# Weight sums of a coming FFN made in the preceding mixer or PLE gate, second-stage tiles among them

## What is computed

```python
for i in range(DEPTH):                                  # DEPTH = 2
    x = x + 0.5 * swiglu(rmsnorm(x, norm_ffn[i, 0]), w_ffn_gate_up[i, 0], w_ffn_down[i, 0])
    h = rmsnorm(x, norm_mix[i])
    mix = even_mixer(h, ...) if i % 2 == 0 else odd_mixer(h, ...)
    x = x + mix
    x = x + 0.5 * swiglu(rmsnorm(x, norm_ffn[i, 1]), w_ffn_gate_up[i, 1], w_ffn_down[i, 1])
    gate = sigmoid(rmsnorm(x, norm_ple[i]) @ w_ple_gate[i])
    x = x + gate * rmsnorm(p[i] @ w_ple_proj[i], norm_ple_proj[i])
y = rmsnorm(x, norm_final)
```

## Time and profile before

| | us |
|---|---|
| median of three runs | 2645.11 |
| profiled execution | 2654.71 |
| its span, slowest core (2) | 2653.2 |
| spans of the eight cores | 2618.6 to 2653.2 |
| PE busy | 2448.4 (92%) |
| DVE busy | 1805.2 (68%) |
| ACT busy | 1009.9 (38%) |
| POOL busy | 977.4 (37%) |
| mean granted clock of PE, by core | 0.954 to 0.967 |

### The profile page before, as it was taken

The page is one execution under the profiler, slowest core; times in us unless marked ns, Lnnn a source line. Parts: engine busy times, 40 slices in busy tenths (PEclk is TensorE's granted clock), DMA queues, the critical chain, the costliest instruction groups (busy, mean ns, idle before and its releaser), DMA issues.

```text
span 2653.2 us, 36263 instructions; the slowest of 8 cores (2618.6 to 2653.2 us)
## 1 busy us (share of the span) xinstructions
PE 2448.4 (92%) x13362; PEld 1165.4 (44%) x13449; DVE 1805.2 (68%) x2922; ACT 1009.9 (38%) x1767; POOL 977.4 (37%) x1006
## 2 busy tenths in 40 slices
PE   7788879999998999899898998999999999999997
PEld 3233434545443444454443444454444444455443
DVE  6889664765676687377785776476566868666677
ACT  3233321444762334044551433143333513423344
POOL 1476875211225656530034746510003256211100
PEclk9899989999999999999999999999999999999887
DMA  7585688663455879965055779953311566755513
GB/s 144 123 194 125 117 183 200 151 141 79 113 130 114 180 166 205 209 164 109 7 129 135 174 171 207 208 129 65 62 38 21 116 147 155 172 128 128 110 21 131
DMA packets 115570, 351.57 MB, mean 133 GB/s; under 512 B 15936, under 2 KB 31296, under 8 KB 115264
## 3 DMA queue, kind: packets, MB, share of 16 engines
q0 software_dynamic: 47088, 163.21, 36.9%
q1 hardware_dynamic: 67584, 184.92, 21.5%
q10 hardware_dynamic: 720, 1.11, 0.1%
HBM read 426.51 MB, written 75.63 MB: 189 GB/s over the span
## 4 chain that ended last, share of the span: by engine, by line
PE 61%; DMA 13%; DVE 13%; POOL 6%; issue 3%; ACT 3%; SPq 0%; POOLq 0%; DVEq 0%; ACTq 0%
PE ps L614 61%; DMA stg<-wts 8%; POOL ringh L580 3%; DMA ringh<-wts 3%; DVE scr L577 3%; DVE hh L584 2%; DVE hih L577 2%; POOL stg L580 2%; DMA x<-xT 1%; DVE h L584 1%; ACT scr L571 1%; DVE x L584 1%; DMA ringh<-wsum 1%; DVE ht L577 1%; ACT L569 1%
## 5 line engine op out<-in xcount | busy, mean ns | idle before, releaser
L571 ACT ACTIVATE scr<-ps 128x512 f32<-128x512 f32 (+1 forms) x814 | 436.2, 543 | 743.9 <-PE ps L614 725.2
L614 PE MATMUL ps<-hh,ringh 128*128 128x512 f16 (+1 forms) x3744 | 691.9, 337 | 2.4 <-DMA ringh<-wts 1.8
L614 PE MATMUL ps<-ht,ringh 128*128 128x512 f16 x2016 | 485.3, 387 | 46.3 <-DVE scr L577 17.5
L584 DVE SCALAR_TENSOR_TENSOR x<-ps,x 128x512 f32<-128x512 f32 (+1 forms) x512 | 322.6, 638 | 301.8 <-PE ps L614 300.9
L614 PE MATMUL ps<-h,ring 128*128 128x512 bf16 (+1 forms) x2379 | 478.9, 356 | 19.1 <-DVE scr L584 6.4
L614 PEld LDWEIGHTS ps<-hh,ringh 128*128 128x128 f16 x3744 | 328.2, 99 | 328.4 <-issue 21.0
L580 POOL TENSOR_TENSOR ringh<-ringh 128x512 f16<-128x512 f16 (+2 forms) x300 | 417.0, 1391 | 99.5 <-DMA ringh<-wts 65.5
L577 DVE TENSOR_TENSOR scr<-ps,scr 128x512 f32<-128x512 f32 x525 | 352.2, 681 | 145.4 <-PE ps L614 135.4
L614 PE MATMUL ps<-hih,ringh 128*128 128x512 f16 x1408 | 343.0, 392 | 61.6 <-DMA ringh<-wts 47.8
L577 DVE TENSOR_TENSOR hih<-ps,scr 128x512 f16<-128x512 f32 x352 | 242.5, 689 | 154.9 <-PE ps L614 130.5
L614 PEld LDWEIGHTS ps<-h,ring 128*128 128x128 bf16 x2420 | 221.8, 100 | 260.3 <-issue 47.2
(11 more groups left out here) (118 smaller groups left out, 1759.0 us busy)
## 6 DMA issues: line engine op xcount, KB each, us to landing
ringh<-wsum SPq DMA_DIRECT2D x125, 512.0 KB, 6.9
ringh<-wts POOLq DMA_DIRECT2D x125, 384.0 KB, 7.0
ringh<-wts POOLq DMA_DIRECT2D x51, 512.0 KB, 7.2
stg<-wts POOLq DMA_DIRECT2D x45, 512.0 KB, 9.4
wsum<-stg SPq DMA_DIRECT2D x45, 512.0 KB, 6.4
wsum<-ringh SPq DMA_DIRECT2D x35, 512.0 KB, 3.4
ringh<-wts POOLq DMA_DIRECT2D x16, 768.0 KB, 8.4
wsum<-ringh SPq DMA_DIRECT2D x16, 768.0 KB, 5.3
```

What stands on the lines that cost most here:

```text
L571: return e.activation(out=out, in_=in_, func=func, **kw)
L584: S.op("dve", lambda e: e.scalar_tensor_tensor(out=out, in0=in0, scalar=scalar, in1=in1, op0=op0, op1=op1), reads=rd, writes=[out])
L614: ins = e.matmul(o_, l, r, start=st, stop=sp, skip_group_check=cont)
```

## The change

The presum moves from the second passes into the even mixer (for FFN 01), the PLE gate of layer 0 (for FFN 10) and the odd mixer (for FFN 11). It works in place, in pieces of 256 or 512 columns of each quarter, in small buffers of the arena that is idle there: per partition two of 2 KB behind the `pt` tiles in the even mixer, three of 4 KB over `ht` in the odd mixer, and three of 4 KB in the hidden arena in the gate. The store of a piece is two transfers, by POOL in the even mixer and by SP elsewhere. `EARLY` now holds gate/up tiles 0 to 7, second-stage tiles among them, then the rest. `pump` stops at a tile whose presum is under way; `close` issues at once what is left of the running pieces. `thold` also holds T(0) in the odd mixer. The norms that waited 145 model us wait 30. The raw phase's tail is deferred by 3.7 instead of 1.5 model us, and the norms of blocks 2 to SB ahead of FFN 00 use mode "pe".

```diff
...
@@ -430,8 +430,9 @@
...
-    STAGE = [at(f"stg{b}", [128, 4096], F16, HAR[b], HB[b]) for b in range(2)]
-    EARLY = list(range(7)) + list(range(8, 22, 2)) + list(range(7, 22, 2))
+    EARLY = [("gu", m) for m in range(8)] + [("dn", 0, 0), ("dn", 0, 1)] + [("gu", m) for m in range(8, 22, 2)]
+    EARLY += [("dn", 1, 0), ("dn", 1, 1)] + [("gu", m) for m in range(9, 22, 2)]
+    EARLY += [("dn", 0, 2), ("dn", 1, 2), ("dn", 0, 3), ("dn", 1, 3)]
...
+    STAGES = {
+        "even": [at(f"stge{i}", [128, 1024], F16, "zone", zo + 4096 + i * 2048) for i in range(2)],
+        "odd": [at(f"stgo{i}", [128, 2048], F16, "zone", zone + i * 4096) for i in range(3)],
+        "ple": [at(f"stgp{i}", [128, 2048], F16, "hid", hid0 + HTB + NHH * 1024 + i * 4096, True) for i in range(3)],
+    }
...
@@ -661,6 +663,9 @@
...
+            self.begun = {}
+            self.partial = {}
+            self.opened = False
...
@@ -677,6 +682,8 @@
         def pump(self, limit=1 << 20):
             while self.pos < min(limit, self.cap):
                 k = self.order[self.pos]
+                if stored(k) in self.begun:
+                    return
                 pl = self._place(k)
                 if pl is None:
                     return
@@ -694,7 +701,7 @@
                     n3, so = n * 3 // 4, sum_off[stored(k)]
...
-                        extra=tuple(extra) + (self.kept[stored(k)],))
+                        extra=tuple(extra) + tuple(self.kept[stored(k)]))
...
@@ -711,30 +718,68 @@
...
-                self.kept[stored(k)] = dma("sp", d_ws[:, so:so + n], t[:, 3 * q:7 * q], f"ssem{pl[0]}")
-
-        def presum(self, keys, side, stop):
-            if not keys or pe_t[0] > stop:
+                self.kept[stored(k)] = [dma("sp", d_ws[:, so:so + n], t[:, 3 * q:7 * q], f"ssem{pl[0]}",
+                                             extra=tuple(self.partial.get(stored(k), ())))]
+
+        def presum(self, name, l, f, pace, lat, op_t, eng):
+            stages = STAGES[name]
+            w = stages[0].shape[1] // 4
+            pieces = []
+            for key in EARLY:
+                k = key[:1] + (l, f) + key[1:]
+                q = wt_off[k][1] // 4
+                pieces += [(k, c, min(w, q - c), c + w >= q) for c in range(0, q, w)]
+            self.opened = True
+            self.next_piece(name, pieces, 0, pace, lat, op_t, eng)
+
+        def next_piece(self, name, pieces, i, pace, lat, op_t, eng):
+            while pieces and pieces[0][1] == 0 and self.order.index(pieces[0][0] + (0,)) < self.pos:
+                k = pieces[0][0]
+                pieces = [p for p in pieces if p[0] != k]
+            if not pieces or not self.opened:
                 return
-            k, t0 = keys[0], pe_t[0]
+            (k, c, cw, end), t0 = pieces[0], pe_t[0]
+            side = i % len(STAGES[name])
+            if c == 0:
+                self.begun[k] = []
             off, n = wt_off[k]
-            q = n // 4
-            a = [STAGE[side][:, j * q:(j + 1) * q] for j in range(4)]
-            r = [STAGE[side][:, n + j * q:n + (j + 1) * q] for j in range(4)]
-            ops = ((r[1], a[0], a[3], ALU.subtract), (r[0], a[3], a[2], ALU.add),
-                   (r[2], r[0], a[0], ALU.subtract), (r[3], a[1], r[2], ALU.subtract))
-            dma("pool", STAGE[side][:, 0:n], d_w[:, off:off + n], f"stgl{side}")
-            for i, (d, x, y, op) in enumerate(ops):
-                at_time(t0 + 7.0 + 1.3 * i, lambda d=d, x=x, y=y, op=op: pool_tt(d, x, y, op), ("early",))
+            st = STAGES[name][side][:, 0:4 * cw].rearrange("p (j c) -> p j c", j=4)
+            a = [st[:, j, :] for j in range(4)]
+            dma("pool", st, d_w[:, off:off + n].rearrange("p (j c) -> p j c", j=4)[:, :, c:c + cw], f"stgl{name}{side}")
+            ops = ((a[2], a[3], a[2], ALU.add), (a[3], a[0], a[3], ALU.subtract),
+                   (a[0], a[2], a[0], ALU.subtract), (a[1], a[1], a[0], ALU.subtract))
+            for x, (d, y, z, op) in enumerate(ops):
+                at_time(t0 + lat + op_t * x, lambda d=d, y=y, z=z, op=op: pool_tt(d, y, z, op), ("early",))
 
             def store():
                 so = sum_off[k]
-                self.kept[k] = dma("sp", d_ws[:, so:so + n], STAGE[side][:, n:2 * n], f"stgs{side}")
-            at_time(t0 + 11.5, store, ("early",))
-            at_time(t0 + 8.0, lambda: self.presum(keys[1:], 1 - side, stop), ("next",))
+                dst = d_ws[:, so:so + n].rearrange("p (j c) -> p j c", j=4)[:, :, c:c + cw]
+                sem = f"stgs{name}{side}"
+                tot = S.dma_cnt.get(sem, 0) + 2
+                for h in range(2):
+                    tk = dma(eng, dst[:, 2 * h:2 * h + 2, :], st[:, 2 - 2 * h:4 - 2 * h, :], sem, total=tot)
+                    self.begun[k].append(tk)
+                if end:
+                    self.kept[k] = self.begun.pop(k)
+            at_time(t0 + lat + 4 * op_t, store, ("early",))
+            at_time(t0 + pace, lambda: self.next_piece(name, pieces[1:], i + 1, pace, lat, op_t, eng), ("next",))
+
+        def close(self):
+            self.opened = False
+            ev = sorted(p[:2] for p in pend if p[2] == ("early",))
+            todo = {p[:2]: p for p in pend if p[2] == ("early",)}
+            pend[:] = [p for p in pend if p[2] != ("early",)]
+            heapq.heapify(pend)
+            for e in ev:
+                todo[e][3]()
+            self.partial.update(self.begun)
+            self.begun.clear()
 
         def get(self, key):
             self.pump()
+            if key not in self.loaded:
+                self.close()
+                self.pump()
...
@@ -1115,7 +1156,7 @@
...
-            defer(1.5, tail, ("tail",))
+            defer(3.7, tail, ("tail",))
...
@@ -1129,9 +1170,6 @@
             ensure(("T", p))
             if p:
                 ensure(("n", SB))
-                if (l, f) != (1, 1):
-                    nl, nf = (l, 1) if f == 0 else (1, 0)
-                    W.presum([("gu", nl, nf, m) for m in EARLY], 0, pe_t[0] + 125.0)
             for pi, part in enumerate(HPARTS):
                 h = len(part) // 2
                 fin = pi == len(HPARTS) - 1
@@ -1148,7 +1186,7 @@
...
-                    nm = {b: Norm(b, gnext, "pe" if p else "dve", None if p else 4.0, 0.0 if p else 145.0)
+                    nm = {b: Norm(b, gnext, "pe" if p else "dve", None if p else 4.0, 0.0 if p else 30.0)
                           for b in PAIRS[p]}
...
@@ -1211,6 +1249,7 @@
 
     def even_mixer(gnext):
         thold.add(0)
+        W.presum("even", 0, 1, 6.5, 5.0, 0.9, "pool")
...
@@ -1284,6 +1323,7 @@
...
                     if b == SB:
+                        W.close()
                         thold.discard(0)
                         try_T(0)
                 defer(3.0, ln1, tag)
@@ -1433,6 +1473,8 @@
                 W.done(("pp",))
 
     def odd_mixer(gnext):
+        thold.add(0)
+        W.presum("odd", 1, 1, 9.0, 7.0, 1.3, "sp")
         for t in XSCR:
             sfree(t)
         dve_memset(ZTAIL[:, :, :], 0.0)
@@ -1478,10 +1520,16 @@
         wo = out_tiles("outo")
         for b in range(SB - 1):
             out_proj([b], YC, wo, gnext)
+            if b == 1:
+                W.close()
+                thold.discard(0)
+                try_T(0)
         out_proj([SB - 1, SB], YC, wo, gnext, "outo")
 
     def ple(l, gnext):
         wp = kview(W.get(("plep", l)), 2)
+        if l == 0:
+            W.presum("ple", 1, 0, 7.0, 7.0, 1.3, "sp")
         order = [(mo, b) for b in range(2) for mo in range(3)] + [(mo, b) for b in range(2) for mo in range(3, 8)]
         order += [(mo, 2) for mo in range(8)] + [(mo, b) for mo in range(8) for b in (3, SB)]
         nm = {}
@@ -1539,7 +1588,7 @@
         at_time(33.0 + 0.8 * c, lambda c=c: raw[1].chunk(c), ("raw", 1))
     for i, (b, c) in enumerate((b, c) for b in range(2, NB) for c in range(8)):
         at_time(75.0 + 3.0 * i, lambda b=b, c=c: load_x(b, c, (last_pe[0],)), ("x", b))
-    n0 = [Norm(b, "norm_ffn00", "dve", 2.0) for b in range(NB)]
+    n0 = [Norm(b, "norm_ffn00", "pe", 2.0) for b in range(NB)]
     for b in range(2, NB):
         for mo in range(8):
             at_time((105.0, 130.0, 155.0)[b - 2] + 2.0 * mo, lambda b=b, mo=mo: n0[b].chunk(mo, 0.0), ("n", b))
```

More of the change, by code:

```diff
@@ L36 @@
 NRUNIT = 72
-ZBYTES = 12288
+ZBYTES = 13056
 PCOL = {}
@@ L530, in ensure @@
         busy[0] = False
-    def settle(kind):
-        while any(p[2] and p[2][0] == kind for p in pend):
-            heapq.heappop(pend)[3]()
     def starved():
@@ L819, in add @@
                     d = {512: 2.5, NSAMP: 9.0}[n] if self.mode == "dve" else 8.0
-                    if self.later:
-                        ensure_early = lambda: (settle("early"), stats(sq))
-                        defer(self.later, ensure_early, self.tag)
-                    else:
-                        defer(d, lambda: stats(sq), self.tag)
+                    defer(self.later or d, lambda: stats(sq), self.tag)
             def stats(sq):
```

## The result

The changed kernel took 2673.62 us in the median of six runs (2669.25 to 2740.65), the kernel before 2650.89 us in the median of six beside it. The ratio is 1.011 (95% interval 1.006 to 1.017), so it is about 1.1% slower, where 2592 us and a gain had been forecast.

A forecast was written before the change was run, and what follows sets the result against it. PE was taken as the bound, with idle time in single stages to win. The sum 2653.2 - 76 - 12 - 7 - 3 + 11 + 16 + 16 + 2 gave 2600.2 us of span, forecast time 2592 us, range 2560 to 2634.

The forecast's parts named there:

- rival B: Even mixer: POOL's queue makes the kernel slower than before, each piece waiting 4.2 us; 2658 to 2716 us, 4% chance.
- (1): Second passes: taking the presum out of them gains 76 us, bounds 65 and 85.
- rival C: Second passes: FFN 11 is no true twin, their loss is moved bytes, half of 76 stays; 2630 us, 6% chance.
- (4), even mixer: Even mixer: 29 presum pieces in POOL's queue cost 16 us, bounds 0 and 45.
- (4), gate: PLE gate: 48 POOL sums slow the DVE through the shared port, cost 16 us, bounds 3 and 28.
- (4), odd mixer: Odd mixer: 84 sums beside a DVE busy 162 of 253 us cost 2 us, bounds 0 and 10.
- rival A: Mixers, gate and first passes: port and queue costs reach their upper ends, 108 instead of 45; 2655 us, 12% chance.
- (2): First passes of FFN 01 and 10: summing second-stage tiles ahead removes waits, gain 12 us, bounds 0 and 19.
- (3): First passes: the number and order of kept tiles cost 4 us in FFN 01 and 7 us in FFN 10.
- (5): Ahead of FFN 00: norms of blocks 2 to 4 on PE relieve DVE, gain 7 us, bounds 0 and 12.
- (6): Raw tail 2.2 us later, so DVE need not stand for the Silu: gain 3 us, from -3 to 5.
- D, the clock: Denser work brings another 200 us stretch at granted clock 0.81, so 38 us return; 2630 us, 8% chance.

The follow-up runs named there:

- e7: Kernel before with its presum kept in the second passes but slowed: first sums 13 us after the load, every second tile only; 2590.77 us, ratio 0.978.
- e8: Changed kernel with every piece loaded and stored but its four POOL sums left out, for timing alone; 2595.21 us in one run.
- after: The changed kernel itself, set against the kernel before; 2673.62 us in the median of six runs, ratio 1.011.
- e1: Changed kernel with all three presum calls removed, in the first group at lower granted clocks; 2851.3 us beside 2850.17 for the kernel before.

## Why the prediction was wrong

The sign was wrong, and the place was rival B's, POOL's queue in the even mixer, which had 4%. The 2670.57 us of the profiled execution lie between its lower end (2658) and its middle (2680), but that agreement is luck: B had POOL wait 4.2 us a piece for its load. It waited 46.5 us for the loads of 29 pieces, 1.6 us each, or 2.0 with the stores, just what the forecast itself had put in. What B and the forecast both missed is how POOL's time reaches PE. Point by point:

- **What bounds the kernel, and (1): right.** The second passes gave 83 us without FFN 11 (40.3 + 20.8 + 22.2), inside 65 to 85; even the 6 us that I left in FFN 00 for its raw tiles came back (40.3 of 41.0). The twin was a twin, so rival C is out. But I took from it that the presum had to *leave* the passes. The second passes of FFN 01 and 10 in e7 show that it was enough to ask for the sums later, and for fewer of them: the first was due 7 us after a load that lands after 9.4. I had both numbers and read them as a reason for the move and not as the fault.
- **(4), even mixer: the step that failed.** 16 us, with 45 as the upper bound, against 77 measured (236.7 to 314.1 from the last `hts` to FFN 01's first product). The sum had three faults of size. The stage was taken as 211 us, 13 of them FFN 01's; it has 198. I priced an issue at 0.57 us, from `ringh`; the pieces' loads and stores took 0.77 and 0.73. A sum of 256 columns, taken as 0.67, has a median of 0.67 and a mean of 0.74. A piece thus costs 5.2 us and not 4.4, which is 151 and not 127 us. With the right sizes my own sum, 127 + 44 + 58 - 211 = 18 us too much, would have been 151 + 43 + 57 - 198 = 53. The rest is a fault of reasoning: I let "what the buffers hide" take from the excess, and nothing add to it. The trace has 151 + 38 + 57 us and 30 more in which POOL was idle for other reasons, 276 in all. Once POOL was late, its lateness was not divided among buffers; it passed on to `sq`, `ptail` and `ht` in turn, 59 us of PE waits, and PE's busy time grew by 24 us at a granted clock of 0.88. My bound was built from an average share ("81% full"), though I had written that behind these pieces stand the very operations PE waits for.
- **(4), gate: right.** 26 us in the stage (143.9 to 170.1) against 16, bounds 3 to 28. e8 gives nearly all of it back (148.5), so with 48 sums it is 0.5 us a sum, between my 0.4 and 0.8. PE's waits for DVE `scr` rose from 10.0 to 28.0 us there.
- **(4), odd mixer: failed.** 20 us in the stage (290.3 to 310.3) against 2 (bounds 0 to 10). I had excused it by DVE's idle time, 91 of 253 us. But 84 sums beside it made DVE's busy time 57.7 us longer (161.8 to 219.6), and its operations are partly a chain that PE waits for: the longest wait for DVE `h` grew from 4.3 to 11.1 us. e8 has 161.2 us of DVE there, and the 21 us are back. It is rival A's mechanism, at twice its size.
- **(2): failed.** 12 us forecast, and as much lost at one place as won at another. FFN 01's wait fell from 4.76 to 1.44 us, but in FFN 10 a wait of 5.29 us (before 5.38) stands at a second-stage tile whose sums POOL brings late, and FFN 11 has a new one of 4.42 us. It was the lower bound that I named: the wait moves on. The rows, PE's timeline of after:

```profile
866.14 1.47 PE L616 MATMUL ps<-hit,ringh 128*128 128x512 f16 x6 [1.44 <-DMA ringh<-wsum]
...
1562.84 4.45 PE L616 MATMUL ps<-hit,ringh 128*128 128x512 f16 x10 [5.29 <-POOL ringh L582]
...
2300.14 2.31 PE L616 MATMUL ps<-hih,ringh 128*128 128x512 f16 x5 [4.42 <-DMA ringh<-wts]
```

- **(3)** put +11 for fewer and differently ordered kept tiles. It did not come: from the first product to the first `hts`, the first passes of FFN 01, 10 and 11 changed by +1.2, -4.3 and +1.6 us. (2) and (3) together were forecast at -1 and measured at -1.5, two misses that cancel.
- **(5) and (6): right in place and, together, in size.** DVE's load in 162 to 245 us fell from 78.4 to 68.6 us. On core 2 the first `hts` came only 3 us earlier, but in the mean of the eight cores 14 us (294.4 to 280.6), and some 12 over all traces, against 7 + 3.
- **D, the clock: did not come.** The second passes ran at 1.00 in `after` on all eight cores, PE busy in 174 of 175 us between 1015 and 1190, and the stretch at 0.81 was gone. The Trainium skill (TensorE: Matmul & The Clock Gate, on the peak-current limiter) has a die at 13/16 of its clock when three of its cores run dense products; this trace disagrees for these passes. The first group of runs comes nearer to it: in e1 cores 0 to 3 had 0.82 to 0.84 in their second passes, cores 4 to 7 had 0.87 or 0.88. What decides between the two is open.

The sum again with what was measured in `after`, core 2, in the order start, second passes, even mixer, gate, odd mixer, first passes, and the part that ran at 0.81 before: -3 - 83 + 77 + 26 + 20 - 1.5 - 20 = +16 us of span, against -10 - 76 + 16 + 16 + 2 - 1 = -53 us forecast. Of the 69 us between the two the even mixer makes 61, the odd mixer 18 and the gate 10; the 0.81 of the kernel before, which has no term in the forecast, takes 20 off.

Left open: how much of the even mixer's loss is queue and how much port, and how the 36 us that stay without sums (278 against 242) divide; what sets the clock in FFN 00's second pass, which took 200 to 221 us in the later-timed versions, the longest at 0.86; and whether, with fewer pieces and later sums, the gate's and odd mixer's place could pay at all. A presum there that runs when DVE does no two-tile operations was not tried.

## What to carry to other kernels

When work is moved into a queue that feeds the bound engine, add up that queue's whole stage: pieces, issues at their own price, waits for their own loads, and the work already there. See that the window of the stage ends where the stage ends. If the queue's work passes the stage's length, price the excess in full on the path at least (here 53 us, and it cost 77); a backlog finds every buffer, and closing one gives little. And before moving work away from where it hurts, look whether it only asks for its data too early: here a load of 9.4 us was wanted after 7, and asking later, with fewer tiles, was worth 2.2% where the move cost 1.1%.

## What the runs showed of the hardware

- **An issue is not one price.** POOL took 0.53 to 0.58 us to issue a ring load, 0.57 for a stage tile of 512 KB in the old passes, but 0.77 and 0.73 us for the `stge` loads and stores, which move parts of rows.
- **DVE and POOL slow each other, with a price.** In the odd mixer DVE's two-tile form took 1102 instead of 752 ns in the mean over 26, in the gate single ones up to 1745 instead of 753 ns, and POOL's `stgo` sums went up to 3539 ns, with a median of 1162. The Trainium skill (GPSIMD Engine Reference, § 1 Specifications) says that the two share their SBUF interfaces and contend when a DVE instruction has two SBUF inputs. This trace agrees: leaving out the sums gave back about 0.5 us a sum in the gate (23 us for 48) and 0.25 in the odd mixer (21 us for 84).
